# The start of a decoder block rearranged: x first and in quarters, row vectors and angles later

## The reference, cut to what matters

```
h = rmsnorm(x, ln1_w)                     # x: 256 x 2048
proj = h @ w_in                           # 2048 x 12816; the q, k, v columns of the
                                          # sliding-window branch come first in the kernel
q = rope(rmsnorm(q_head, q_norm_w), positions)   # 12 heads of 128
k = rope(rmsnorm(k_head, k_norm_w), positions)
```

## Time and profile before

| | us |
|---|---|
| median of 3 runs | 1512.86 (1512.79 to 1513.46) |
| the profiled execution | 1512.96 |
| its span, first to last instruction | 1511.2 |
| mean granted TensorE clock | 0.998 of full |
| PE busy | 1501.3 (99% of the span) |
| DVE, ACT, POOL busy | 1109.9, 797.8, 94.1 |

### The profile page before, as it was taken

One profiled execution on the slowest core, in us unless ns is written; L12 is line 12 of the kernel. 1 busy time (PEld: TensorE's weight loads), 2 busy tenths in 40 slices (PEclk: granted clock), 3 DMA queues, 4 the chain that ended last, 5 costly groups with the idle time before them and its releaser, 6 DMA issues.

```text
span 1511.2 us, 19446 instructions
## 1 busy us (share of the span) xinstructions
PE 1501.3 (99%) x7484; PEld 1266.0 (84%) x7484; DVE 1109.9 (73%) x1318; ACT 797.8 (53%) x900; POOL 94.1 (6%) x129
## 2 busy tenths in 40 slices
PE   9999999999999999999999999999999999999999
PEld 7888888888888888888888888888888888888887
DVE  5878756878777877776655566688977566678988
ACT  6554444676654544454444545455545444456664
POOL 5000000000040100100000101100000111110000
PEclk9999999999999999999999999999999999999999
DMA  8578897744544444445656656656566666666874
GB/s 290 196 260 295 301 355 261 244 148 166 169 166 155 143 149 139 139 150 184 242 177 193 188 182 189 192 195 210 181 213 204 195 185 187 186 216 242 300 289 149
DMA packets 150087, 310.74 MB, mean 206 GB/s; under 512 B 7681, under 2 KB 8193, under 8 KB 148225
## 3 DMA queue, kind: packets, MB, share of 16 engines
q1 hardware_dynamic: 148752, 307.65, 60.9%
q10 hardware_dynamic: 1264, 2.13, 0.4%
HBM read 295.09 MB, written 14.68 MB: 205 GB/s over the span
## 4 chain that ended last, share of the span: by engine, by line
PE 93%; DVE 4%; issue 1%; DMA 1%; ACT 0%; SPq 0%; DVEq 0%; ACTq 0%
PE banks L564 43%; PE banks L922 16%; PE banks L990 11%; PE banks L968 9%; PE banks L925 8%; PE banks L580 2%; DVE lo L1474 1%; DVE lo L2085 1%; PE banks L828 1%; DMA raw<-in_w_ff 1%; PE banks L703 1%; PE banks L676 1%; DVE diag L1493 1%; PE banks L819 1%; DMA x_tok<-in_x 0%
## 5 line engine op out<-in xcount | busy, mean ns | idle before, releaser
L1474 DVE TENSOR_TENSOR lo<-raw,hi 128x1024 fp32r<-128x1024 f32 x384 | 473.7, 1238 | 285.5 <-ACT hi L1023 283.1
L1023 ACT ACTIVATE hi<-raw 128x1024 fp32r<-128x1024 f32 x383 | 404.8, 1059 | 437.1 <-PE banks L564 263.1
L564 PE MATMUL banks<-hi,st 128*128 128x512 f32 x1600 | 504.1, 396 | 1.6 <-DVE gates L1818 1.6
L564 PEld LDWEIGHTS banks<-hi,st 128*128 128x128 f32 x1600 | 292.5, 188 | 58.0 <-DVE gates L1818 1.4
L922 PE MATMUL banks<-st,hi 128*128 128x512 f32 x1024 | 321.6, 395 | 0.0
L564 PE MATMUL banks<-lo,st 128*128 128x512 f32 x800 | 312.1, 390 | 0.0
L925 PEld LDWEIGHTS banks<-st,lo 128*128 128x128 f32 x1024 | 192.4, 188 | 45.4
L1424 ACT ACTIVATE hi<-raw 128x1024 fp32r<-128x1024 f32 x136 | 144.3, 1062 | 122.5 <-PE banks L990 89.0
L925 PE MATMUL banks<-st,lo 128*128 128x256 f32 x1024 | 201.2, 278 | 0.0
L2085 DVE TENSOR_TENSOR lo<-raw,hi 128x1024 fp32r<-128x1024 f32 x136 | 164.9, 1223 | 32.9 <-ACT hi L1424 28.2
L564 PEld LDWEIGHTS banks<-lo,st 128*128 128x128 f32 x800 | 150.2, 188 | 32.1
(11 more groups left out here) (296 smaller groups left out, 1633.3 us busy)
## 6 DMA issues: line engine op xcount, KB each, us to landing
raw<-in_w_ff SPq DMA_DIRECT2D x122, 1024.0 KB, 5.2
raw<-in_w_in SPq DMA_DIRECT2D x99, 1024.0 KB, 5.0
raw<-in_w_out SPq DMA_DIRECT2D x16, 1024.0 KB, 5.2
early_sum<-in_w_ff SPq DMA_DIRECT2D x12, 1024.0 KB, 7.3
w_sums<-early_sum SPq DMA_DIRECT2D x12, 1024.0 KB, 9.1
raw<-w_sums SPq DMA_DIRECT2D x12, 1024.0 KB, 5.1
raw<-in_w_gdn_proj SPq DMA_DIRECT2D x8, 1024.0 KB, 5.1
raw<-in_w_swa_proj SPq DMA_DIRECT2D x4, 1024.0 KB, 5.0
```

The lines of the kernel that those rows point to most:

```text
L564: last = pe.matmul(acc[:, t], w[:, k0 + 2 * m + kk, P * t:P * t + P], v[:, (i + more) % PIECES, kk, :], start=m == 0 and kk == 0 and a == ...
L1023: act.activation(hi[:, (i + more) % PIECES], raw[:, i // 2 % RAW, 2 * (i % 2):2 * (i % 2) + 2, :], ACT.Copy)\
L1474: dve.tensor_tensor(lo[:, (i + more) % PIECES], raw[:, i // 2 % RAW, 2 * (i % 2):2 * (i % 2) + 2, :], hi[:, (i + more) % PIECES].bitcast(F ...
```

## The change

x arrives in four quarters, each on its own semaphore, the first ahead of every other transfer of SP; the other quarters stand one by one ahead of weight tiles 1, 2 and 3. The three row vectors are issued by ACT's queue, ahead of the positions and frequencies. PE turns ln1_w alone, then the first quarter with one signal for each chunk, and only then ln2_w, conv_w and the residue products; the dummy products become 2 of 512 and 2 of 256 columns. The second quarter is turned behind place 0 of group 0 (with a wait for chunk 1 in the middle of place 0), the third behind place 4, the fourth behind place 8. ACT and DVE split piece 0 behind chunk 0, pieces 1 and 2 behind chunk 3, piece 3 behind chunk 7. DVE computes the angles at pieces 6 and 8 of its list and the mask and columns in group 1. The first table set is now that of Ln and Exp; the trig set is loaded behind group 0's readouts, then the sine, then the other set again. DVE builds the rope tables in the chain of group 0. The low parts of pieces 4 and 5 of group 1 are made inside that chain, and q's turn and its store move from place 7 to place 13 (store: from piece 4 to piece 7) of group 1. POOL's mask work waits for the last chunk of x.

```diff
-FIRST_SPLITS = {1: 0, 3: 1, 5: 2, 7: 3}
-WARM = (3, 5)
+FIRST_SPLITS = {0: (0,), 3: (1, 2), 7: (3,)}
+WARM = (2, 2)
...
+        def x_turned(k):
+
+            if k < 4:
+                return wk[:, k, 0:TT * P]
+            at = (0, 2, 0)[k // 4 - 1] + k % 4 // 2
+            return wk[:, at, TT * P * (k % 2):TT * P * (k % 2) + TT * P]
...
+            def x_quarter(n):
+                sp.dma_start(x_tok[:, :, N * n:N * n + N], x_v[:, :, N * n:N * n + N]).then_inc(ev[f"x_in{n}"], 16)
+
+            x_quarter(0)
             sp.dma_start(raw[:, 0, 0:2], w_in_v[:, 0:2, span(COL_SWA, N)]).then_inc(ev["w_first"], 16)
             sp.dma_start(raw[:, 0, 2:4], w_in_v[:, 2:4, span(COL_SWA, N)]).then_inc(landed[0], 16)
...
-            tile(0, 1, w_in_v, 4, COL_SWA, first=True)
-            sp.dma_start(x_tok[:, :, D // 2:D], x_v[:, :, D // 2:D]).then_inc(ev["x_right"], 16)
-            tile(0, 2, w_in_v, 8, COL_SWA, first=True)
-            tile(0, 3, w_in_v, 12, COL_SWA, first=True)
+            for j in range(1, 4):
+                x_quarter(j)
+                tile(0, j, w_in_v, 4 * j, COL_SWA, first=True)
...
+                                if kk and place == 0 and second is not None:
+                                    second()
...
-            pe.wait_ge(ev["w_rows"], 48)
-            pe.transpose(wk[:, 4, 0:2 * KC], rows[0:2 * KC, 0, :], ident[0:2 * KC, 0:2 * KC])
+            pe.wait_ge(ev["ident_made"], 4)
+            pe.wait_ge(ev["w_ln"], 16)
+            pe.transpose(wk[:, 4, 0:KC], rows[0:KC, 0, :], ident[0:KC, 0:KC]).then_inc(ev["rows_turned"], 1)
+
+            def first_turn(n):
+                pe.wait_ge(ev[f"x_in{n}"], 16)
+                for b in range(4):
+                    for t in range(TT):
+                        last = pe.transpose(x_turned(4 * n + b)[:, P * t:P * t + P], x_tok[:, t, N * n + P * b:N * n + P * b + P], ident[:])
+                    if b == 3 or n == 0:
+                        last.then_inc(ev["x_turned"], 1)
+
+            first_turn(0)
+            pe.wait_ge(ev["cols_made"], 1)
+            pe.wait_ge(ev["w_rows"], 32)
+            pe.transpose(wk[:, 4, 2 * P:2 * P + KC], rows[32:32 + KC, 0, :], ident[32:32 + KC, 32:32 + KC])
             pe.transpose(wk[:, 4, P:P + 96], rows[0:96, 1, :], ident[0:96, 0:96]).then_inc(ev["rows_turned"], 1)
             pe.wait_ge(ev["res_made"], 1 + NG)
             for g, dil in enumerate(DILS):
                 last = pe.matmul(wk[:, 5, P * g:P * g + P], res_ind[0:dil, g, :], res_ind[0:dil, g, :],
                                  start=True, stop=True)
             last.then_inc(ev["res_product"], 1)
-
-            def first_turn(n):
-                at = (0, 2, 4, 0)[n]
-                dst = wk[:, at:at + 2, :].rearrange("p a (b t) -> p (a b) t", t=TT * P)
-                turn(lambda t, b: x_tok[:, t, N * n + P * b:N * n + P * b + P], dst, ev["x_turned"])
...
-            pe.wait_ge(ev["x_left"], 16)
-            first_turn(0)
-            first_turn(1)
             warm(WARM[1], 2)
             pe.sem_inc(piece_used, PIECES)
             pe.sem_inc(acc_free, TT)
-            pe.wait_ge(ev["x_split_lo"], 2)
+            pe.wait_ge(ev["x_split_lo"], 1)
+
+            def second_turn():
+                first_turn(1)
+                pe.wait_ge(ev["x_split_lo"], 4)
...
-                    group(g, g, 8, st_hi, st_lo, mid={0: x_chunks(4)},
-                          after={1: third_turn, 2: fourth_turn, 3: x_chunks(12), 5: x_chunks(16)})
+                    group(g, g, 8, st_hi, st_lo, second=x_chunks(2), mid={0: second_turn, 2: third_turn, 4: fourth_turn},
+                          after={1: x_chunks(8), 3: x_chunks(12), 5: x_chunks(16)})
                 else:
-                    group(g, g, 8, st_hi, st_lo, after={3: a_turn(g - 1)} if g <= 6 else {})
+                    after = {6 if g == 1 else 3: a_turn(g - 1)} if g <= 6 else {}
+                    group(g, g, 8, st_hi, st_lo, after=after)
...
-            act.preload_act_table_set("trig_and_small")
+            act.preload_act_table_set("natural_log_exp_and_others")
+            act.dma_start(rows[0:KC, 0, :], ln1_w.rearrange("(k p) -> k p", p=P)).then_inc(ev["w_ln"], 16)
+            act.dma_start(rows[32:32 + KC, 0, :], ln2_w.rearrange("(k p) -> k p", p=P)).then_inc(ev["w_rows"], 16)
...
             for k in range(KC // 2):
                 first_hi(k)
-                if k == 1:
+                if k == 0:
                     act.wait_ge(piece_used, PIECES)
                     act.wait_ge(ev["w_first"], 16)
                     act.activation(hi[:, 0], raw[:, 0, 0:2, :], ACT.Copy).then_inc(hi_ready, 1)
                 elif k in FIRST_SPLITS:
-                    split(0, FIRST_SPLITS[k])
+                    for i in FIRST_SPLITS[k]:
+                        split(0, i)
...
             def sines():
+                act.wait_ge(ev["angles"], 13)
+                act.preload_act_table_set("trig_and_small")
...
+                if n == 0:
+                    sines()
...
-                    steps = {1: right_hi(2), 2: right_hi(3), 3: x_sum(0), 4: x_sum(1), 5: sines, 6: x_factor}
+                    steps = {1: right_hi(2), 2: x_sum(0), 3: right_hi(3), 4: x_sum(1), 5: x_factor}
                 else:
-                    steps = {4: a_store((n - 1) % 2, (n - 1) // 2, n - 1)}
+                    steps = {7 if n == 1 else 4: a_store((n - 1) % 2, (n - 1) // 2, n - 1)}
...
-            def a_post(w, n):
+            def a_post(w, n, between=()):
+                if n == 0:
+                    tables()
...
+                if between:
+                    between[0]()
...
+                if between:
+                    between[1]()
...
-                    steps = {1: right_lo(2), 2: right_lo(3), 3: angles, 4: angles_in, 6: tables}
+                    steps = {1: right_lo(2), 2: angles, 3: right_lo(3), 4: angles_in}
+                elif n == 1:
+                    steps = {3: columns}
                 elif n == 2:
                     steps = {3: ab_split}
                 else:
                     steps = {}
-                ahead(QA + n, 8, steps, more_steps=lambda m, n=n: stored_sums(8 * n + m))
-                a_post(n % 2, n)
+                ahead(QA + n, 8, steps, more_steps=lambda m, n=n: stored_sums(8 * n + m), m0=2 if n == 1 else 0)
+                a_post(n % 2, n, [lambda m=m: split(QA + 1, PIECES + m) for m in range(2)] if n == 0 else ())
```

More of the change, by code:

```diff
@@ L454, in _ @@
             pool.memset(ident[:], 0.0).then_inc(ev["ident_made"], 1)
-            pool.memset(ones[:], 1.0).then_inc(ev["ones_made"], 1)
-            pool.memset(tri[:], 1.0).then_inc(ev["tri_made"], 1)
+            pool.memset(ones[:], 1.0).then_inc(ev["ident_made"], 1)
+            pool.memset(tri[:], 1.0).then_inc(ev["ident_made"], 1)
             pool.memset(res_ind[:], 0.0).then_inc(ev["res_made"], 1)
@@ L546, in _, with group @@
         def _(pe):
-            def group(q, g, n, sth, stl, i0=0, k0=0, mid={}, after={}, more=0, banks_read=None):
+            def group(q, g, n, sth, stl, i0=0, k0=0, mid={}, after={}, more=0, banks_read=None, second=None):
                 place = 0
@@ L1061, in read_out @@
                 return first, second
-            act.preload_act_table_set("trig_and_small")
+            act.preload_act_table_set("natural_log_exp_and_others")
+            act.dma_start(rows[0:KC, 0, :], ln1_w.rearrange("(k p) -> k p", p=P)).then_inc(ev["w_ln"], 16)
+            act.dma_start(rows[32:32 + KC, 0, :], ln2_w.rearrange("(k p) -> k p", p=P)).then_inc(ev["w_rows"], 16)
+            act.dma_start(rows[0:96, 1, :], conv_w.rearrange("j (b p) -> (j b) p", p=P)).then_inc(ev["w_rows"], 16)
             with nc.allow_non_contiguous_dma(reason="256 positions"):
@@ L1069, in first_hi @@
             def first_hi(k):
[L1070 to L1071 removed]
+                act.wait_ge(ev["x_turned"], k + 1 if k < 4 else k // 4 + 4)
+                src = x_turned(k)
                 act.activation(st_hi[:, k], src, ACT.Copy, scale=lncol[:, k:k + 1]).then_inc(ev["x_split_hi"], 1)
@@ L1095, in step @@
                 def step():
+                    for n in range(4):
+                        act.wait_ge(ev[f"x_in{n}"], 16)
                     f(x_scr[:], x_tok[:, t], ACT.Square, (ev["x_square"], t) if t else None, ev["x_square"],
@@ L1215, in ab_chain @@
                 f(tmpc, tmpc, ACT.Ln, (ev["ab_act"], 4), ev["ab_act"], bias=1.0)
-                f(ea_c, alog_c, ACT.Exp, (ev["w_head"], 48), ev["ab_act"])
+                f(ea_c, alog_c, ACT.Exp, (ev["w_bcast"], 80), ev["ab_act"])
             def ob_hi_step():
@@ L1475, in split, with ahead @@
                                   hi[:, (i + more) % PIECES].bitcast(F32), ALU.subtract).then_inc(lo_ready, 1)
-            def ahead(q, n, steps={}, i0=0, read_out=(), more=0, then=None, more_steps=None):
-                for m in range(n):
+            def ahead(q, n, steps={}, i0=0, read_out=(), more=0, then=None, more_steps=None, m0=0):
```

(31 more changed lines are left out.)

26 lines of the change are left out of this document (8 added, 18 removed).

## The result

| | before | after |
|---|---|---|
| median of 14 runs each (us) | 1512.75 (1511.42 to 1514.35) | 1516.11 (1513.9 to 1518.12) |
| ratio, with its 95% interval | | 1.0023 [1.0016, 1.003] |
| the profiled execution | 1512.96 | 1515.97 |
| its span | 1511.2 | 1514.3 |
| its mean granted clock | 0.998 | 0.996 |

The changed kernel is 3.4 us slower (1516.1 us); 1511.1 was forecast. PE is busy for as long as before, so the time is in waits and in a slow clock, not in work.

A forecast was written before the change was run, and what follows sets the result against it. PE bounds the kernel, so only its start could pay: 6.1 - 0.9 - 0.9 = 4.3 us earlier, less 2.25 and 0.15 in group 1, 1.9 us gained on 1512.96: 1511.1, range 1508.9 to 1514.5.

The forecast's parts named there:

- The landing of x: At the launch: first quarter of x lands at 5.5 us, ends 4.7 and 7.5; tile 1 at 12.0.
- The row vectors. Cost nothing: On ACT's queue, conv_w lands at 5.7 to 6.5, before PE needs it at 6.6; cover about 0.3 us.
- rival (e): At the start, conv_w lands late and holds PE: whole gain gone at 9, 1516.0 and more from 13; chance 0.05.
- the sum for the start: Landing, turn, scaling and splits let group 0 start at 9.2 us, 6.1 us earlier.
- The clock: In group 0, PE at half clock until 11, between 9.6 and 13.3; 1.8 us at half, costing 0.9.
- rival (b): Start: clock at half until 14.5 or x lands at 7.5; 0.3 gained to 1.7 lost (1512.7 to 1514.7); chance 0.17.
- the wait at place 9: In group 1, PE ready at 12.25 waits for piece 5's low part at 14.5: 2.25 us.
- The comparison: Start of group 1, set against before's profile with group 0 ending at 39.2: 4.3 us earlier, at 34.5.
- The table loads: In ACT's chain behind group 0, two loads, each 1.28 us, next instruction 1.29 after the start.
- Rival (d): In the chain, a load holds ACT for twice 1.28; 2.6 us more at place 9, 1513.7; chance 0.05.
- The turn moved into the group: The second quarter's turn, formerly ahead of group 0, now stands in it: 0.9 us lost.
- The 0.15 at place 13: In group 1, columns and mask on DVE make piece 7 ready at 20.1 against 20.0: 0.15 us wait.

The follow-up runs named there:

- rows late: Changed kernel with ln2_w, conv_w and residue products turned behind place 3 of group 0: 1515.05 us; with more dummy products at the start too, 1514.28.
- kernel without tables: Changed kernel without both table loads behind group 0 and a copy in place of the sine: 1514.36 us, ratio 1.0019.
- wait filled: Changed kernel with dummy products of 512, 512 and 256 columns behind place 8 of group 1: 1514.38 us, ratio 1.0017.
- chain alone: Kernel before with only the change's table loads, sine, low parts of pieces 4 and 5 and q's turn moved: 1516.17 us, ratio 1.0025.
- the same with its wait filled: Kernel before with the change's chain part, plus dummies of 512, 512 and 256 columns behind place 8 of group 1: 1515.24 us, ratio 1.002.
- dense start: Kernel before with three more dummy products of 256 columns ahead of its wait for x: 1512.10 us, ratio 0.9999.
- reordering: Changed kernel with low parts of pieces 4 and 5 ahead of all rope products, mask columns moved to group 3: 1513.87 us, ratio 1.0008.
- start alone: Changed kernel given back the chain of before, so only the new start remains: 1513.12 us, ratio 1.0001.
- start alone with rows late: New start with before's chain, ln2_w and conv_w turned behind place 3 of group 0, dense dummies from 1.2 to 9.3 us: 1510.87 us, 0.9987.

## Why the prediction was wrong

**The landing of x: right.** The quarter had landed at 5.35; 5.5 was taken. Tile 1 came at 13.5 instead of 12.0, which cost nothing while PE itself was late (with the rows late it ended a wait of 0.2 to 0.5 at place 4).

**"The row vectors. Cost nothing": wrong, and the first step that failed.** conv_w landed at 7.8, not at 5.7 to 6.5, and took 6.0 us instead of 3.9. This is rival (e), at the small end of its range. The prediction counted on a cover of 0.3 us and took the duration from a row in which conv_w went before x; now it went beside x and the weights. ln1_w and ln2_w took 4.0 instead of 1.7. From conv_w's issue to its landing the core's 16 DMA engines were busy for 0.92 of the time and moved 286 GB/s, where before they were busy for 0.56 and moved 90. No run here sends the rows from ACT's queue without bulk transfers beside them, so how much is the queue's own isn't shown, and that the rows share the engines with the bulk is the prediction's own guess at the cause. With the wait, and with the rows, the residue products and the two dummies at half clock behind it, group 0 started at 11.6 instead of 9.2. About 1 us of these 2.4 is the half clock: in the kernel without tables conv_w landed as late (7.9), the clock stood at 1.00 up to 10.6, and the first product came at 10.65. The kernels with the rows late started at 9.3 to 9.4, so the sum for the start was right but for this item.

**"The clock": wrong twice.** Before's record has it at half from about 7.7 to 14.5. In the changed kernel's profile it also fell at 7.7, and came back at 14.5 and not at 11, as rival (b) had it, so that 2.9 us of group 0 ran at half, 1.5 lost instead of 0.9. No run shows the forecast's term of 0.9, 1.8 us of group 0 at half up to 11: where the record has the fall at the start, the clock came back at 13.2 to 15.0. And in group 1 it fell again. The prediction priced the wait at place 9 at its own length (2.25, measured 2.34: right) and put nothing for a clock behind it, although it had just priced one behind a gap of PE at the start. The fall cost 1.4 us (8.54 against 7.13 with the wait filled). Of the five traces with this wait of 2.3 us unfilled, three have the fall (8.54 to 8.74 for 30 matmuls) and two don't (7.10 and 7.12). A slip on the way: the 1.7 lost of rival (b) counts the half clock to 14.5 as if group 0 still started at 9.2; with x at 7.5 it starts 2 us later, and the loss is 0.9 (1513.8).

**The comparison: wrong, and not seen at all.** The gain of the start was worked out against one profiled execution, whose own clock had fallen. Three traces of the old start without a fall (chain alone, the same with its wait filled, dense start) end group 0 at 37.4 to 37.6 and not at 39.27. Up to 1.7 of the forecast 4.3 us was thus the difference between executions of the same kernel. Over many runs before's clock averages 0.9990, so such a fall is part of some executions and not of others. The dense start moves the trace by 1.9 (71.05 against 72.91) and the median by only 0.3: it removes a fall that only part of before's executions have, and the interval allows up to 1.5. How much of the 1.7 counts in the medians is thus not shown.

**The table loads: right.** Load, sine, load and square start 1.29, 0.44 and 1.29 apart (39.51, 40.80, 41.24, 42.53). The load itself took 1.28, so the trace shows nothing on top of it, also where two different sets follow one another. Rival (d) falls.

**The small items.** The turn moved into the group cost its 0.87. The 0.15 at place 13 wasn't seen; the wait moved by the reordering was 1.55, where 1.4 was expected.

**The sum made again** with the measured terms, against a kernel before without a fall: start 37.83 - 37.5 = 0.3 lost, wait 2.3, lead-in 0.3, clock 1.4, together 4.3. In the other traces of this wait the clock's part is missing in two of five, so 2.9 to 4.3; measured 3.4 [2.4, 4.5]. The experiments say where it sits: the chain's half alone loses 3.4 us, the start's half 0.4, which its interval doesn't tell from nothing. The sign hung on the start: of the 4.3 forecast, the late first product took 2.4, the longer half clock in group 0 0.6, which leaves the 1.4 of the two profiles (1.3 by this sum), and the comparison took 1.7.

## What to carry to other kernels

Before a gain is read off a profile, see whether the profiled execution is like the others, by the duration of equal matmuls and not by the recorded clock alone: a clock at half for a few microseconds moved the start here by 1.7 us. Price a wait of TensorE at its length and the clock that may fall behind it (here 2.3 us and, in three of five traces, 1.4 to 1.6 more), and prefer an order that leaves no wait to one that fills it. A small transfer that everybody waits for isn't free on a second queue (6.0 us here against 3.9): have nobody wait for it early, rather than send it early.

## What the hardware showed that I had not expected

- A stretch of 2.3 us without matmuls, behind a group and a half of unbroken ones, brought the clock to half in three traces (8.54, 8.70, 8.74 us for the 30 matmuls behind it) and not in two (7.10, 7.12). In both traces with the wait filled by dummy products it didn't fall (7.13, 7.13). With the changed kernel's start it fell at 7.7, 8.2, 9.8 or 10.6, by trace; with before's start at 7.7 in one trace and not at all in two.
- The recorded clock can lack a slow stretch: start alone has 1.00 from the first instruction on, while two products took 1.42 us at 11.75 and 0.70 at 14.85.
- With wide dummy products in the gaps of the start, the recorded clock was 1.000 in 11 of 11 runs, twice (start alone with rows late; dense start); in the profiled executions the durations agree (12 dummy instructions of 256 columns in 2.75 us, 6 in 1.56, where 4 took 2.08 at half). Without them the kernel before averages 0.9990.
- 48 KB in 96 rows took 6.0 us on ACT's queue beside bulk transfers, and 3.9 on SP's queue ahead of them.
- What stays open: why the same wait lowers the clock only in some executions, how much of the rows' 6.0 us is due to their queue, and what sets the late landing at 171 us and the waits behind 1360 us.
